# Reordering the front of a state-space, pooling, convolution and FFN layer: first loads, weight buffer sets, and the place of thirty projection blocks

## The reference, cut to what matters

```python
h = rmsnorm(x, norm1_g) * (1 + sc1) + sh1          # sh1, sc1, ... = silu(c) @ ada_w + ada_b
z = h @ w_in                                       # 1152 tokens x 1024 -> 1280 columns
u_ssm, u_pool, u_conv = z[:, :512], z[:, 512:768], z[:, 768:]
# both directions: state scan of u_ssm (32 groups x 64 complex), D term, gelu, GLU
# windows 2, 4, 8, 16 over u_pool, minus the token, times pool_w
# GLU of u_conv, depthwise convolution of width 31, layer norm, swish
x = x + g1 * (concat(y_ssm, y_pool, y_conv) @ w_out)
x = x + g2 * ffn(rmsnorm(x, norm2_g) * (1 + sc2) + sh2)
```

## Time and profile before

| | us |
|---|---|
| runs shown (median of 3) | 1330.0 (1328.51 to 1331.0) |
| profiled execution, span from first to last instruction | 1323.8 |
| median of the runs less that span | 6.2 |
| PE busy in the span | 1220.8 (92%) |
| DVE busy | 850.8 (64%) |
| POOL busy | 516.0 (39%) |
| ACT busy | 511.0 (39%) |
| first 439 us | front; the rest is the FFN |

### The profile page before, as it was taken

How to read it: one execution, slowest core, us unless ns; L and a number is a source line. 1 busy time by engine, 2 the same in 40 slices (tenths; PEclk the granted TensorE clock), 3 DMA queues, 4 the chain that set the end, 5 groups by cost and what they waited for, 6 DMA issues and landing times.

```text
span 1323.8 us, 21436 instructions
## 1 busy us (share of the span) xinstructions
PE 1220.8 (92%) x7574; PEld 1080.5 (82%) x7574; DVE 850.8 (64%) x1338; ACT 511.0 (39%) x911; POOL 516.0 (39%) x360
## 2 busy tenths in 40 slices
PE   6786978995599999899999999999999999999996
PEld 4486877895545788799999999999889999999995
DVE  5538539959973427677666667766865555555558
ACT  2652531117235646633333333333532333334223
POOL 0595104376233101654444455444443233333340
PEclk9897988898799999999999999999999999999998
DMA  8815054389791331866665766666768777777771
GB/s 308 339 64 157 28 163 150 105 95 211 204 400 64 128 112 64 270 225 221 206 217 187 246 222 227 217 207 220 260 193 276 246 256 256 260 254 263 244 275 75
DMA packets 189570, 268.52 MB, mean 203 GB/s; under 512 B 14031, under 2 KB 108537, under 8 KB 186825
## 3 DMA queue, kind: packets, MB, share of 16 engines
q1 hardware_dynamic: 188144, 263.07, 60.6%
q0 software_dynamic: 1280, 4.72, 0.9%
q10 hardware_dynamic: 88, 0.02, 0.0%
HBM read 186.49 MB, written 81.26 MB: 202 GB/s over the span
## 4 chain that ended last, share of the span: by engine, by line
PE 76%; DMA 5%; issue 4%; POOL 4%; ACT 4%; DVE 3%; SPq 3%; DVEq 0%; ACTq 0%; POOLq 0%
PE banks L862 22%; PE banks L864 22%; PE banks L863 22%; PE banks L1131 3%; DMA ad<-in_ada_w 1%; PE banks L898 1%; PE banks L947 1%; SPq L436 1%; ACT nts L1660 1%; PE banks L1013 1%; POOL psum_w L751 1%; POOL sst L791 1%; DMA z_dram<-zp 1%; POOL pu L757 1%; PE banks L1136 1%
## 5 line engine op out<-in xcount | busy, mean ns | idle before, releaser
L814 POOL TENSOR_TENSOR raw13r<-raw13s,w13h 128x512 fp32r<-128x512 f32 x110 | 155.1, 1418 | 467.1 <-ACT w13h L1612 421.9
L863 PE MATMUL banks<-ntr,w13h 128*128 128x256 f32 (+1 forms) x1144 | 336.1, 294 | 0.0
L862 PE MATMUL banks<-ntr,w13h 128*128 128x256 f32 (+1 forms) x968 | 282.5, 292 | 4.4 <-ACT xs L1622 2.3
L863 PEld LDWEIGHTS banks<-ntr,w13h 128*128 128x128 f32 x1144 | 215.5, 188 | 0.9
L862 PEld LDWEIGHTS banks<-ntr,w13h 128*128 128x128 f32 x968 | 182.5, 189 | 6.5 <-ACT xs L1622 2.6
L862 PE MATMUL banks<-f2h,f_hi 128*128 128x512 f32 x396 | 156.6, 395 | 0.4 <-DVE acc L2317 0.4
L864 PE MATMUL banks<-f2h,f_lo 128*128 128x512 f32 x396 | 156.2, 395 | 0.0
L863 PE MATMUL banks<-f2l,f_hi 128*128 128x512 f32 x396 | 156.2, 394 | 0.0
L864 PE MATMUL banks<-ntr,raw13r 128*128 128x256 f32 (+1 forms) x528 | 153.5, 291 | 0.0
L2183 DVE TENSOR_TENSOR acc<-acc,banks 128x512 f32<-128x512 f32 x170 | 112.7, 684 | 38.9 <-PE banks L864 30.8
L818 POOL TENSOR_TENSOR f2l<-f2s,f2h 128x1024 fp32r<-128x1024 f32 x44 | 106.1, 2432 | 34.1 <-ACT f2h L1616 34.1
(11 more groups left out here) (323 smaller groups left out, 2536.4 us busy)
## 6 DMA issues: line engine op xcount, KB each, us to landing
raw13s<-in_ffn_w SPq DMA_DIRECT2D x66, 512.0 KB, 4.5
parts<-w13h SPq DMA_DIRECT2D x110, 256.0 KB, 2.4
w13h<-parts SPq DMA_DIRECT2D x110, 256.0 KB, 2.7
f2s<-in_ffn_w SPq DMA_DIRECT2D x44, 512.0 KB, 4.2
ad<-in_ada_w SPq DMA_DIRECT2D x20, 1024.0 KB, 9.8
parts<-wsumr SPq DMA_DIRECT2D x66, 256.0 KB, 2.6
wsumr<-parts SPq DMA_DIRECT2D x55, 256.0 KB, 4.9
parts<-raw13r SPq DMA_DIRECT2D x44, 256.0 KB, 2.9
```

The costliest lines, as they stand in the source:

```text
L814: nc.gpsimd.tensor_tensor(w13_low(x, f), w13_low(x, f, F32), w13h[x][:, :, :].bitcast(F32), ALU.subtract).then_inc(sem("w13_lo"), 1)
L862: nc.tensor.matmul(out, hi_w, hi_x, start=start, stop=False)
L863: nc.tensor.matmul(out, hi_w, lo_x, start=False, stop=False)
```

## The change

It touches the program of every engine ahead of the projection's end, and the two places behind it that count the same semaphores (no work is changed there).

1. Start. On SP the first two ada tiles come right after three small loads, ahead of the four tables and the positions; the token tiles and the other ada tiles follow in another order; weight tiles 0, 1 and 2 are loaded without a wait. Four small loads (two states, `rtap`, `dn`) move to the end of ACT's list.
2. A third set of weight buffers. Tiles 0, 1, 2 take sets 0, 1, 2, and tile i from 3 on the set in `W_SLOT`, whose tile before is `W_PRIOR[i]`. The low parts of tiles 0 and 1 move from DVE to POOL (around the first `wc_piece`), DVE keeps 2, 3 and 4, at other places.
3. DVE adds the positions of tiles 4, 5 before `gsc` and of 6, 7 behind step 7; ACT sums the squares of tiles 4 to 7 behind step 7 and not between steps.
4. PE's order: turns 2 to 7, blocks 0, 1, turns 8 to 17, block 2, and as before up to block 5; blocks 6 to 8 follow at once, then `wb_turn` in two pairs around blocks 9 to 11; `state_inputs` in two pairs around block 12; then block 13, and four times block, ade half, block, kb half, ade half, kb half; eight blocks remain.
5. SP's and ACT's programs follow that order.

```diff
...
+    W_SLOT = (0, 1, 2, 0, 1, 0, 1, 0, 1, 0)
+    W_PRIOR = (None, None, None, 0, 1, 3, 4, 5, 6, 7)
+    LOW_POOL = (0, 1, 5, 6, 7, 8, 9)
...
-        return (sem("w_in_lo"), i + 1) if i < POOL_LOW else (sem("w_in_lo_pool"), i + 1 - POOL_LOW)
+        return (sem("w_in_lo_pool"), LOW_POOL.index(i) + 1) if i in LOW_POOL else (sem("w_in_lo"), i - 1)
...
-        for i, name in enumerate(("ssm_lam_re", "ssm_lam_im", "state_ssm_re", "state_ssm_im")):
+        for i, name in enumerate(("ssm_lam_re", "ssm_lam_im")):
             sp.dma_start(rlam[:, i, :], dview(A[name], 0, [[P, Q], [1, P]])).then_inc(sem("vectors_in"), 16)
-        sp.dma_start(rtap[:, :], dview(A["conv_dw_w"], 0, [[P, 2 * TAPS], [1, P]])).then_inc(sem("vectors_in"), 16)
-        sp.dma_start(dn[:, :], dview(A["ssm_d"], 0, [[32, NPAIR], [1, 32]])).then_inc(sem("vectors_in"), 16)
+        ada_in(0)
+        ada_in(1)
         for i, name in enumerate(("ssm_b_re", "ssm_b_im", "ssm_c_re", "ssm_c_im")):
             sp.dma_start(raw[i][:, :], dview(A[name], 0, [[2048, Q], [1, 2048]])).then_inc(sem("raws_in"), 16)
         sp.dma_start(pos_c[:, :], A["pos_cols"]).then_inc(sem("pos_in"), 16)
         sp.dma_start(pos_r[:, :], A["pos_rows"]).then_inc(sem("pos_in"), 16)
-        for n in range(4):
-            x_in(n)
-            ada_in(n)
+        x_in(0)
+        ada_in(2)
+        x_in(1)
+        ada_in(3)
+        x_in(2)
+        x_in(3)
         ada_in(4)
         ada_bias(0)
         sp.wait_ge(sem("raws_turned"), 3)
         for n in range(5, KT):
             ada_in(n)
+        x_in(4)
+        x_in(5)
         w_in_load(0)
-        for i in range(4, 8):
+        w_in_load(1)
+        for i in range(6, 9):
             x_in(i)
-        w_in_load(1)
-        x_in(8)
+        w_in_load(2)
         sp.dma_start(edge[:, :], A["pool_edges"]).then_inc(sem("edges_in"), 16)
         for i in range(8):
             sp.wait_ge(sem("pos_half"), 2 * (i + 1))
             sp.dma_start(dview(x2_dram, i * P * D, [[D, P], [1, D]]), xt[i][:, :]).then_inc(sem(f"x_saved{i // 4}"), 16)
+            if i == 3:
+                sp.wait_ge(*low_ready(0))
+                w_in_load(3)
+        sp.wait_ge(*low_ready(1))
+        w_in_load(4)
...
+        for i in range(2):
+            z_saved(i)
+            sp.wait_ge(sem("z_out"), 16 * (i + 1))
+            u_first(i)
+        z_saved(2)
+        sp.wait_ge(*low_ready(3))
+        w_in_load(5)
+        z_saved(3)
+        sp.wait_ge(sem("z_out"), 64)
+        for i in range(2, 4):
+            sp.wait_ge(sem("v_done"), 8 * (i - 1))
+            u_first(i)
+        sp.wait_ge(*low_ready(4))
+        w_in_load(6)
...
+        w_low(0)
         pool.wait_ge(sem("gsc"), 1)
-        pool.wait_ge(sem("w_in_lo"), 1)
         pool.wait_ge(sem("powers"), 1)
         pool.wait_ge(sem("cc_evac"), 2)
-        for n in range(8):
+        wc_piece(0)
+        w_low(1)
+        for n in range(1, 8):
             wc_piece(n)
+        w_low(5)
...
-        x_turns(2, 5)
+        x_turns(2, 4)
         pos_row(6)
-        x_turns(5, 7)
         pos_row(7)
-        x_turns(7, 10)
+        x_turns(4, 8)
...
-            if s < 3:
+            if s < 1:
                 pe.wait_ge(sem("mod_evac"), 1)
+            elif s < 3:
                 pe.wait_ge(sem("pos_half"), 16)
...
         z_block(0)
-        x_turns(10, 13)
         z_block(1)
-        x_turns(13, 18)
+        x_turns(8, 18)
         z_block(2)
         x_turns(18, 21)
         z_block(3)
         x_turns(21, 24)
-        z_block(4)
-        z_block(5)
+        for s in range(4, 9):
+            z_block(s)
         wb_turn(0)
-        for s in range(6, 9):
-            z_block(s)
         wb_turn(1)
-        wb_turn(2)
         for s in range(9, 12):
             z_block(s)
+        wb_turn(2)
         wb_turn(3)
-        for j in range(4):
-            state_inputs(j)
+        state_inputs(0)
+        state_inputs(1)
         z_block(12)
+        state_inputs(2)
+        state_inputs(3)
+        z_block(13)
         pe.wait_ge(sem("bblk"), 2)
         pe.wait_ge(sem("dsel"), 1)
         pe.wait_ge(sem("z_evac"), 10)
-        for m in range(8):
-            z_block(13 + m)
-            ade_half(m)
-            kb_half(m // 2, m % 2)
-        for s in range(21, 30):
+        for n in range(4):
+            z_block(14 + 2 * n)
+            ade_half(2 * n)
+            z_block(15 + 2 * n)
+            kb_half(n, 0)
+            ade_half(2 * n + 1)
+            kb_half(n, 1)
+        for s in range(22, 30):
             z_block(s)
...
         for dst, src in SMALL:
             act.dma_start(dst(), src()).then_inc(sem("vectors_in"), 16)
+        for i, name in enumerate(("state_ssm_re", "state_ssm_im")):
+            act.dma_start(rlam[:, 2 + i, :], dview(A[name], 0, [[P, Q], [1, P]])).then_inc(sem("vectors_in"), 16)
+        act.dma_start(rtap[:, :], dview(A["conv_dw_w"], 0, [[P, 2 * TAPS], [1, P]])).then_inc(sem("vectors_in"), 16)
+        act.dma_start(dn[:, :], dview(A["ssm_d"], 0, [[32, NPAIR], [1, 32]])).then_inc(sem("vectors_in"), 16)
...
+            act.wait_ge(*w_arrived(i))
+            if W_PRIOR[i] is not None:
+                act.wait_ge(sem("z_done"), ZDONE[W_PRIOR[i]])
+            nc.scalar.copy(w_hi[W_SLOT[i]][:, :, :], wst[W_SLOT[i]][:, :, :]).then_inc(sem("w_in_hi"), 1)
...
+        mod_row_out(0, B[4])
         w_high(0)
-        mod_row_out(0, B[4])
         mod_turn_out(0, B[4])
         act.wait_ge(sem("gsc"), 1)
         act.wait_ge(sem("mod_evac"), 1)
         for n in range(KT):
             h_out(n)
-            if n >= 4:
-                square_sum(n)
+        w_high(1)
+        for i in range(4, 8):
+            square_sum(i)
         root(1)
-        w_high(1)
+        z_out(0)
         h_out(KT)
         square_sum(8)
         root(2)
-        for n in range(KT + 1, 13):
+        h_out(KT + 1)
+        z_out(1)
+        for n in range(KT + 2, 16):
             h_out(n)
-        z_out(0)
-        for n in range(13, 16):
-            h_out(n)
-        z_out(1)
+        w_high(2)
...
-        wb_out(0)
         for s in range(6, 9):
             z_out(s)
-        w_high(4)
+        wb_out(0)
         wb_out(1)
-        wb_out(2)
         for s in range(9, 12):
             z_out(s)
+        w_high(5)
+        wb_out(2)
         wb_out(3)
         for j in range(4):
             v_out(j)
-        w_high(5)
         z_out(12)
-        for m in range(8):
-            z_out(13 + m)
-            if m in (1, 4, 7):
-                w_high(6 + m // 3)
-            kb_evac(m // 2, m % 2)
-        for s in range(21, 30):
+        z_out(13)
+        for n in range(4):
+            z_out(14 + 2 * n)
+            if n in (0, 3):
+                w_high(6 if n == 0 else 8)
+            z_out(15 + 2 * n)
+            if n == 1:
+                w_high(7)
+            kb_evac(n, 0)
+            kb_evac(n, 1)
+        for s in range(22, 30):
             z_out(s)
...
+        pos_add(4)
+        pos_add(5)
...
-        w_low(0)
...
-            if n in (0, 1, 3, 5):
-                pos_add(4 + (n + 1) // 2)
             if n == KT - 1:
+                pos_add(6)
+                pos_add(7)
                 dve.wait_ge(sem("pos_half"), 16)
                 inverse_ms(1)
-                w_low(1)
             if n == KT:
                 inverse_ms(2)
+            if n == 2 * KT - 1:
+                w_low(2)
...
-            if j < 3:
-                w_low(j + 2)
+            if j < 2:
+                w_low(j + 3)
...
```

More of the change, by code:

```diff
@@ L165, in build @@
     o += 4096
-    assert o <= O_WS
+    O_W2 = o
+    assert o + 12288 <= O_WS
     o = O_BC + 12288
@@ L182, in build @@
     st = at("st", [P, 2 * Q * SLOTS], O_ST)
-    wst = [at(f"wst{i}", [P, KT, P], O_WS + 4096 * i) for i in range(2)]
-    w_hi = [at(f"w_hi{i}", [P, KT, P], O_WS + 8192 + 8192 * i, F32R) for i in range(2)]
-    w_lo = [at(f"w_lo{i}", [P, KT, P], O_WS + 12288 + 8192 * i, F32R) for i in range(2)]
+    wst = [at(f"wst{i}", [P, KT, P], a) for i, a in enumerate((O_WS, O_WS + 4096, O_W2))]
+    w_hi = [at(f"w_hi{i}", [P, KT, P], a, F32R) for i, a in enumerate((O_WS + 8192, O_WS + 16384, O_W2 + 4096))]
+    w_lo = [at(f"w_lo{i}", [P, KT, P], a, F32R) for i, a in enumerate((O_WS + 12288, O_WS + 20480, O_W2 + 8192))]
     ad0 = [at(f"ad0{i}", [P, 2048], O_NT + 8192 * i) for i in range(KT)]
@@ new lines, in z_saved, with u_first @@
+        def z_saved(i):
+            sp.wait_ge(sem("z_evac"), ZDONE[i])
+            sp.dma_start(dview(z_dram, i * P * CH * UC, [[CH * UC, P], [1, CH * UC]]),
+                         view(zp[i % 2], 0, [[1, CH * UC]])).then_inc(sem("z_out"), 16)
+        def u_first(i):
+            for s in range(CH):
+                sp.dma_start(u8[i % 2][16 * s:16 * s + 16, :, :],
+                             dview(z_dram, i * P * CH * UC + s * UC, [[CH * UC, 16], [16 * CH * UC, 8], [1, UC]])).then_inc(sem(f"u{i}_in"), 16)
@@ new lines, in _ @@
+        for i in range(2):
```

(24 more changed lines are left out.)

61 lines of the change are left out of this document (14 added, 47 removed).

## The result

The change took 1310.26 us (median of 4 runs, 1307.07 to 1315.37) beside 1329.26 for the kernel before (4 runs, 1326.2 to 1331.0): a ratio of 0.9864, 95% interval 0.9833 to 0.9895. By the medians that is 19 us less and not 36. It lies above the range on record, and by the 2% that parts "faster" from "same" it is the same, to which the prediction gave 0.02. The profiled execution of the change had a span of 1310.0, 13.8 under the one before; its own time was 1311.89, so 1.9 us lie around a span. By that, the profiled execution of before was a quick one (1323.8 + 1.9 against a median of 1330.0), and 4.3 of my 6.2 were no distance between span and time.

What follows compares the result with a forecast made beforehand. Front bound by PE's own time, its idle gaps and low-clock stretches. Start and normed tokens -2.7, then -10.9, -10.6 and -12.9 sum to -37: span 1323.8 to 1286.8, plus 6.2 gives 1293 us; range 1281 to 1308.

Steps and rivals of the forecast that it cites:

- my 6.2: Distance in us added to the forecast span of 1286.8, since the median of the runs lay that far above the span.
- The start: Two ada tiles ahead of tables and positions make the scale ready later, at 48.7: +2.6 us, bounds -1.7 and +4.3.
- The normed tokens: Scale to block 2: additions leave DVE's path, blocks 0 and 1 fill a wait; block 2 at 81.6, -2.7 with the start.
- Blocks 6 to 11 and state inputs: Third weight set lets blocks 6 to 8 follow block 5, -10.9 us; more cover for state inputs' data, another -10.6.
- the rule on turns: Turns don't count as PE activity, so blocks behind each pair start at low clock: 3.6 us, 1297; rival, chance 0.04.
- Lag kernels: Block 13 to the projection's end: waits for the lag kernels' weights and low clock go; -12.9 us, bounds -4 and -13.6.
- the 0.2 per pair for ACT's copies: Extra time allowed in each of the four lag kernel pairs, 59.9 us for the four.
- Behind it: After the projection's end all stays as before; the last gate's wait moves along and PE binds, not DVE.
- Small loads late: ACT's thirteen small loads land behind the positions, PE's first turns some 2.4 us later: 1295 to 1297; rival, chance 0.05.
- A wait came back: Lag weights still late, or ACT stands behind a weight tile's copy: +5 to +12, 1298 to 1305; rival, chance 0.20.
- The clock: Denser work from 60 to 263 us gets the low clock, blocks 6.4 us instead of 4.22: 1358; rival, chance 0.03.
- DVE did not bind: DVE's taps would become the bound at -40.7 us; PE binds, by 3.7.

Runs made afterwards that it cites:

- e1: The change with its four small loads moved from ACT's queue back to SP, ahead of the two ada tiles; 1304.84 us.
- e2: The change with only one of the four small loads, the taps `rtap`, back on SP; 1303.01 us.
- e4: The change with SP's program up to the fifth ada tile in the order of the kernel before; 1301.65 us.
- e5: The change with SP's start as before, the last ade half ahead of block 21, and position rows 6 and 7 right behind mod_turn; 1294.27 us.
- e10: The change with the load of the taps moved to the head of ACT's list; 1303.89 us (one run).
- e8: e5 with block 1 put back behind turn 12, as in the kernel before; 1295.38 us.
- e7: The change with the lag kernel stage on PE and ACT in the order of the kernel before; 1330.45 us, ratio 0.9998.
- e3: The change with the last (eighth) ade half put ahead of block 21; 1309.75 us.
- e11: The change with the edits of e10 and e3, and the position rows as in e5; 1298.25 us.

## Why the prediction was wrong

- **The start, +2.6.** This term failed. I let the small vectors have 7.3 us of slack and gave their being late a chance of 0.05 and a price of 2.4. They came 14 us later than before (20.81 against 6.90) and so 5.5 behind where I had put the positions (about 15.3), whose turns they kept waiting. The term measured +13.9 at the scale (60.05 against 46.12), 11.4 more than forecast, and e1, e2 and e4 give 9.6 to 12.0 of it back. The rule of the Trainium skill ("DMA: Bandwidth & Descriptors", Queues, rings and completion order), that an engine alternates between queues by packet, stood in that rival; the trace agrees with it, with one 512-byte row of an engine per 8 KB packet of 0.32 us, and the packet counts give the size: 31 of the taps' 62 rows stand in line on each of two engines. I had priced "slowed" without counting rows. The bound that I took from the trace, PE's 3.98 us of idle time, was no bound on lateness.
- **The normed tokens, -5.3.** Too small as well: from the scale to block 2 the sum had 32.9 us, and the change took 42.0. With the start as before and the position rows out of the way (e5), block 0 came 11.3 us after the scale, for 10.9 in the sum. In the change itself it came 18.0 after it. The position rows 6 and 7 stand between turns, which accounts for some 2.5: in e2 and e10, with the same order on PE and a clock of 1.00, it came 13.6 after the scale. The other 4.4 go with the half clock from 63 to 73. The ten turns of the next group took 15.4 (86.60 to 102.04) and not 12.4 + 1.2: PE waits 2.57 at 92.22 for ACT's rounding, and 94 to 97 is at half clock. They took 15.55 in e5 too, and e8 shows that this is no fault of the missing block.
- **Blocks 6 to 11 and state inputs, -10.9 and -10.6.** Right: -12.2 and -10.9, no wait on `wst`, none on `u`; of PE's 13.3 us of waits on `wb` 3.4 are left. Block 9, behind a pair of turns, opened with 0.42 again and three blocks took 12.75 (142.75 to the next turns at 155.50). For the first pair this speaks against the rule on turns that the prediction cites from the Trainium skill ("TensorE: Matmul & The Clock Gate", Part 4: PE-mode transpose). For the second pair it is open: in e2, e8 and e10 the clock fell to 0.50 for 3.4 us among its turns (in e8 from 144.8), and the stretch to the state inputs took 1.0 more; in the change and the other eight it stayed at 1.00, with the same wait of 1.5 us among the turns.
- **Lag kernels, -12.9.** It was -5.4. The cause that I named was right (e7: 11.6), no wait on `kbw` was left, and the clock was 1.00 up to the last pair. What failed: the 0.2 per pair for ACT's copies was 0.9, since the copy between the two halves ended the overlap of the ade half with the second half; and the order put block 21's evacuation behind a wait that I had not listed, 4.35 (e3). I followed what waits for the moved PE work, but not what ACT waits for between two blocks.
- **Behind it, 0.** About right: from the projection's end to the output projection took 1.7 us less than before. The taps still waited 5.81 us for the first gate; PE did not wait for them.
- **The rivals.** "Small loads late" is what happened, at several times its price. A wait came back, but not one of those named: ACT stood in order behind another. The clock was priced too low: 0.66 from 212 to 222 is a mean, with 0.50 from 213.4 to 220.3, and at 0.50 one matmul of a block follows another after 0.32 us and not 0.18 (from 84.76 to 86.68 in the trace of before), some 7.7 a block and not 6.4. It did not decide the whole, but it took the 4.4 us above. Up to the projection's end the change's clock fell each time behind a wait of PE (1.11 to 2.57 us); e2 and e10 had the same wait of 2.47 behind the scale and kept 1.00, so what made the difference is open. DVE did not bind.

With the three faults taken out (e5) the time is 1294, close to the sum's 1293, and that is luck in part. e5 also gives up the ada tiles in front, its projection ends at 268.2 and not at 262.5, the way from there to the output projection was 2.7 us shorter than before, and its runs lie 1.8 above their spans where the sum added 6.2. With the ada tiles in front and the three faults mended another way (e11) it is 1298.

## What to carry to other kernels

Do not take a load off a queue for the 0.4 us of its issue without asking what its rows will stand beside: a small load with 31 rows on each of two engines, beside 2 MB on another queue, made the first turns 9 us later. When work is moved on one engine, list every semaphore that the in-order programs of its partners wait for between the old place and the new one; one waiting evacuation holds all that stand behind it. And where runs scatter by several us, compare in the traces the length of the stage that was edited. The start of the first untouched stage is a weaker measure: with the same program up to there, the scale came at 60.05 in the change, 60.08 in e3 and 62.03 in e7, block 2 at 102.04, 102.08 and 105.38. Differences in the front under some 3 us need more than one trace.
